# A hybrid retention, sparse-attention and mixture-of-experts layer: experts in order of load, fourteen of them as raw fp32 products on two 64-column tiles

## The reference, cut to what matters

```python
logits = h @ router_w + router_b                 # 512 x 32
top_vals, top_idx = lax.top_k(logits, 4)
gates = softmax(top_vals)
# for every expert e, over the rows (tokens) that chose it:
gu = xb @ w_gu[e] + b_gu[e]                      # 1024 -> 2048
gate, up = jnp.split(gu, 2, axis=-1)
gate = jnp.minimum(gate, 7.0); up = jnp.clip(up, -7.0, 7.0)
glu = gate * jax.nn.sigmoid(1.702 * gate)
y = ((up + 1.0) * glu) @ w_down[e] + b_down[e]   # 1024 -> 1024
# out = x + g2 * segment_sum(y * gate_of_row, token)
```

## Time and profile before

| | us |
|---|---|
| time, median of 3 runs (lowest to highest) | 1501.27 (1499.06 to 1501.77) |
| span of the profiled execution | 1494.1 |
| PE busy | 1459.7 (98%) |
| DVE busy | 1257.1 (84%) |
| ACT busy | 1062.7 (71%) |
| POOL busy | 375.6 (25%) |
| DMA, mean over the span | 318 GB/s |

### The profile page before, as it was taken

One profiled execution on the slowest core, in us unless ns is written; L12 is line 12 of the kernel. 1 busy time (PEld: TensorE's weight loads), 2 busy tenths in 40 slices (PEclk: granted clock), 3 DMA queues, 4 the chain that ended last, 5 costly groups with the idle time before them and its releaser, 6 DMA issues.

```text
span 1494.1 us, 21340 instructions
## 1 busy us (share of the span) xinstructions
PE 1459.7 (98%) x7139; PEld 1149.1 (77%) x7139; DVE 1257.1 (84%) x1146; ACT 1062.7 (71%) x1122; POOL 375.6 (25%) x267
## 2 busy tenths in 40 slices
PE   4999999999999999999999999999999999999997
PEld 1667974567888888888888888888888888888885
DVE  0576765358999999999999999999999999999997
ACT  3542334546887888788888888888788888888883
POOL 1000020203122233322223333222223332222251
PEclk9999999999999999999999999999999999999999
DMA  9655620066899999999999999999999999999994
GB/s 347 214 160 203 223 103 15 27 233 250 344 375 369 375 368 373 370 368 373 371 377 383 370 383 376 372 364 371 374 369 379 373 370 369 377 372 372 384 369 151
DMA packets 95076, 474.96 MB, mean 318 GB/s; under 512 B 23748, under 2 KB 33964, under 8 KB 42816
## 3 DMA queue, kind: packets, MB, share of 16 engines
q1 hardware_dynamic: 82656, 451.39, 78.0%
q0 software_dynamic: 12304, 22.97, 5.5%
q10 hardware_dynamic: 80, 0.13, 0.0%
HBM read 468.16 MB, written 23.09 MB: 329 GB/s over the span
## 4 chain that ended last, share of the span: by engine, by line
PE 92%; DMA 3%; ACT 2%; DVE 1%; issue 0%; SPq 0%; DVEq 0%; ACTq 0%
PE bank L1587 16%; PE bank L1590 15%; PE bank L1594 15%; PE bank L1615 7%; PE bank L1623 7%; PE bank L1616 7%; PE bank L1389 4%; PE bank L1201 3%; PE bank L1203 3%; PE bank L1202 3%; DMA area<-bias_g_parts 2%; PE bank L1563 2%; PE bank L1555 2%; PE bank L1156 1%; PE bank L1362 1%; PE bank L1579 1%
## 5 line engine op out<-in xcount | busy, mean ns | idle before, releaser
L1812 DVE TENSOR_TENSOR e_lo<-ring,e_hi 128x2048 fp32r<-128x2048 f32 x384 | 865.7, 2288 | 62.2 <-ACT e_hi L808 61.3
L808 ACT ACTIVATE e_hi<-ring 128x2048 fp32r<-128x2048 f32 x384 | 728.1, 1920 | 208.3 <-PE bank L1594 207.1
L1587 PE MATMUL bank<-e_hi,x_hi 128*128 128x512 f32 x1024 | 403.7, 394 | 0.0
L1590 PE MATMUL bank<-e_hi,x_lo 128*128 128x512 f32 x1024 | 399.5, 390 | 0.0
L1594 PE MATMUL bank<-e_lo,x_hi 128*128 128x512 f32 x1024 | 274.1, 390 | 0.0
L1587 PEld LDWEIGHTS bank<-e_hi,x_hi 128*128 128x128 f32 x1024 | 192.3, 188 | 46.5 <-issue 7.2
L1594 PEld LDWEIGHTS bank<-e_lo,x_hi 128*128 128x128 f32 x1024 | 192.4, 188 | 40.3
L1590 PEld LDWEIGHTS bank<-e_hi,x_lo 128*128 128x128 f32 x1024 | 192.5, 188 | 39.0
L1615 PE MATMUL bank<-e_hi,act_hi 128*128 128x512 f32 x496 | 196.3, 396 | 0.0
L1616 PE MATMUL bank<-e_hi,act_lo 128*128 128x512 f32 x496 | 193.5, 390 | 0.0
L741 POOL COPY future<-routes 128x1 int32 (+1 forms) x31 | 81.6, 2631 | 366.8 <-DVE area L2116 366.8
(11 more groups left out here) (270 smaller groups left out, 1575.1 us busy)
## 6 DMA issues: line engine op xcount, KB each, us to landing
ring<-in_w_gu SPq DMA_DIRECT2D x256, 1024.0 KB, 9.0
ring<-in_w_down SPq DMA_DIRECT2D x128, 1024.0 KB, 7.2
ring<-in_ada_w SPq DMA_DIRECT2D x24, 1024.0 KB, 9.1
ring<-in_w_in SPq DMA_DIRECT2D x9, 1024.0 KB, 7.9
ring<-in_w_o SPq DMA_DIRECT2D x4, 1024.0 KB, 5.8
xs<-in_x SPq DMA_DIRECT2D x4, 512.0 KB, 4.7
ring<-in_w_in SPq DMA_DIRECT2D x8, 256.0 KB, 5.6
xn_rows<-area POOLq DMA_DIRECT2D x4, 512.0 KB, 5.0
```

What stands on the lines that cost most here:

```text
L808: return nc.scalar.activation(dst, src, ACT.Copy, scale=scale)
L1587: pe.matmul(bank[b][:], x_hi[:, c, :], hi, start=False, stop=False)
L1590: pe.matmul(bank[b][:], x_lo[:, c, :], hi, start=False, stop=False)
L1812: tt(e_lo[c % PARTS][:], raw(period.raw_slot(c)), e_hi[:, c % PARTS, :].bitcast(F32), ALU.subtract).then_inc(lo_ready, 1)
```

## The change

An order of wide (H) and narrow (L) items is written down, and the experts are put into it by load, on the chip.

- Experts 0 and 1 stay first and wide. DVE ranks the other thirty by their count (seven small steps and some more on the tables), PE picks the row lists by rank, SP reads the expert's number of each item from SBUF (TENSOR_LOAD) for its addresses. SP waits for tables_ready before the w_down chunks of expert 0. The 16 heaviest of the thirty are wide, the 14 lightest narrow. Rows of a narrow item past 64 would go to the branch for further items; with the counts above there are none.
- A wide item is computed as before.
- A narrow item takes the raw chunk as it lands: no `hi`, no `lo`. A stationary operand has 64 columns; of two 512-column products one goes to PSUM partitions 0 to 63 and one to 64 to 127 (two column tiles). A w_gu or w_down chunk is 4 fp32 matmuls of 512 columns in place of 12 fp32r ones. A slot of a narrow item is free when PE has used it (chunk_used). The gelu, clip and multiply handle 512 columns instead of 1024, the activations need 4 transposes instead of 8, and ACT moves the upper half of the down sums to partitions 0 to 63 (upper_rows) before rows_out.
- A semaphore bias_used makes SP wait until the bias before was read. The place of up_bias, behind chunk 4, stays.
- The hardware loops over items 2 to 30 are written out on PE, ACT, DVE and SP.

```diff
+ORDER = "HH" + "LHLHLHHLHLHLHHLHLHLHHLHLHHLHLL"
+NARROW = 64
...
             def raw_free(period, c):
 
-                sp.wait_ge(lo_ready, period.at(c) - (SLOTS - 1))
+                before = period.at(c) - SLOTS
+                if isinstance(before, int) and before < MAIN_CHUNKS and not chunk_wide(before):
+                    sp.wait_ge(chunk_used, before + 1)
+                else:
+                    sp.wait_ge(lo_ready, splits_before(before) + 1)
...
-            def up_bias(e):
-
+            def up_bias(i, e):
+
+                if i is not 0:
+                    sp.wait_ge(bias_used, i)
                 for g in range(4):
                     sp.dma_start(bias_g[32 * g:32 * g + 3, :], bias_g_dram[g, e, :, :]).then_inc(g_rows_in, 16)
...
-            def steady(i, e, e_before):
+            def gate_up_chunks(i, e):
                 period = Later(i)
                 for c in range(GU):
                     raw_free(period, c)
                     gu_chunk(period, c, e)
                     if c == 4:
-                        up_bias(e)
+                        up_bias(i, e)
+
+            def down_chunks(i, e_before):
+                period = Later(i)
                 for q in range(DN):
                     raw_free(period, GU + q)
                     down_chunk(period, GU + q, q, e_before)
...
+            e_before, e = 0, 1
+            for i in range(1, E):
+                gate_up_chunks(i, e)
+                if i == 1:
+                    sp.wait_ge(tables_ready, 1)
+                if i + 1 < E:
+                    e_next = sp.value_load(expert_at[0:1, i + 1:i + 2], min_val=0, max_val=E - 1)
+                down_chunks(i, e_before)
+                e_before, e = e, e_next
...
+            def upper_rows(i):
+
+                if not wide(i - 1):
+                    a.wait_ge(chunk_used, Later(i).at(CHUNKS))
+                    copy(upper[0:NARROW, :], bank[4][NARROW:P, :]).then_inc(upper_moved, 1)
...
+            def gate_up_narrow(period):
+
+                i = period.i
+                pe.wait_ge(g_rows_in, i * 64 + 64)
+                pe.wait_ge(xt_taken, i * 2 + 2)
+                pe.wait_ge(up_ready, i)
+                pe.wait_ge(glu_ready, i)
+                for g in range(4):
+                    rows, half = slice(32 * g, 32 * g + 3), slice(NARROW * (g % 2), NARROW * (g % 2) + NARROW)
+                    mm = pe.matmul(bank[g // 2][half, :], ones_b[rows, 0:NARROW], bias_g[rows, :], start=True,
+                                   stop=False)
+                mm.then_inc(bias_used, 1)
+                for c in range(GU):
+                    pe.wait_ge(*period.landed(c))
+                    w = raw(period.raw_slot(c))
+                    for g in range(4):
+                        half = slice(NARROW * (g % 2), NARROW * (g % 2) + NARROW)
+                        mm = pe.matmul(bank[g // 2][half, :], xgT[:, c, 0:NARROW], w[:, 512 * g:512 * g + 512],
+                                       start=False, stop=(c == GU - 1))
+                    mm.then_inc(chunk_used, 1)
+
+            def down_narrow(period, c0, out, turned, between=None):
+
+                i = period.i
+                pe.wait_ge(y_ready, i)
+                pe.wait_ge(ahi_ready, i * 2)
+                for n in range(DN):
+                    pe.wait_ge(*period.landed(c0 + n))
+                    w = raw(period.raw_slot(c0 + n))
+                    for k in range(2):
+                        left = turned[:, 2 * (n % 2) + k, NARROW * (n // 2):NARROW * (n // 2) + NARROW]
+                        for q in range(2):
+                            mm = pe.matmul(out[NARROW * q:NARROW * q + NARROW, :], left,
+                                           w[:, k * D + q * 512:k * D + q * 512 + 512],
+                                           start=(n == 0 and k == 0), stop=(n == DN - 1 and k == 1))
+                    mm.then_inc(chunk_used, 1)
...
-                gate_up(period)
+                if isinstance(i, int) and not wide(i):
+                    gate_up_narrow(period)
+                else:
+                    gate_up(period)
...
+            def order_experts():
+
+                e = slice(0, E)
+                v.wait_ge(order_consts, 1)
+                done(stt(out=load[e, :], in0=dbank(D_["c3"])[e, E:2 * E], scalar=float(E), in1=tie[e, :], op0=ALU.mult,
+                         op1=ALU.add))
+                done(tt(ahead[e, :], load[e, :], ident[e, 0:E], ALU.mult))
+                done(nc.vector.tensor_reduce(my_load[e, :], ahead[e, :], AX.X, ALU.add))
+                done(ts(ahead[e, :], load[e, :], my_load[e, :], None, ALU.is_gt))
+                done(nc.vector.tensor_reduce(my_rank[e, :], ahead[e, :], AX.X, ALU.add))
+                done(ts(chosen[e, :], load_rank[e, :], my_rank[e, :], None, ALU.is_equal))
+                done(ts(is_narrow[e, :], my_rank[e, :], float(N_WIDE), None, ALU.is_ge))
...
+            def mixed(i):
+
                 period, after = Later(i), Later(i + 1)
-                lo(period, 4)
-                lo(period, 5)
-                act_rest(i)
-                for c in range(6, CHUNKS - 1):
-                    lo(period, c)
+                if wide(i):
+                    lo(period, 4)
+                    lo(period, 5)
+                if wide(i - 1):
+                    act_rest(i)
```

More of the change, by code:

```diff
@@ L99, with wide, chunk_wide, splits_before @@
 BESIDE = [1 if 4 <= i < STEPS else 2 if i >= STEPS else 0 for i in range(STEPS + VALUE_LAG)]
+ORDER = "HH" + "LHLHLHHLHLHLHHLHLHLHHLHLHHLHLL"
+NARROW = 64
+assert len(ORDER) == E and ORDER[:2] == "HH" and ORDER[-1] == "L"
+N_WIDE = ORDER.count("H")
+N_NARROW = E - N_WIDE
+assert (N_WIDE - 1) * (CAP + 1) > S * K
+LOAD_RANK = [ORDER[:p].count("H") if m == "H" else N_WIDE + ORDER[:p].count("L") for p, m in enumerate(ORDER)]
+def wide(i):
+    return i >= E or ORDER[i] == "H"
+def chunk_wide(n):
+    i, c = divmod(n + DN, CHUNKS)
+    if n < GU:
+        return wide(0)
+    return wide(i) if i < E and c < GU else wide(i - 1)
+MAIN_CHUNKS = CHUNKS * E
+SPLIT_CHUNKS = [n for n in range(MAIN_CHUNKS) if chunk_wide(n)]
+RAW_CHUNKS = MAIN_CHUNKS - len(SPLIT_CHUNKS)
+def splits_before(n):
+    if isinstance(n, int) and n < MAIN_CHUNKS:
+        return sum(m < n for m in SPLIT_CHUNKS)
+    return n - RAW_CHUNKS
+def wides_before(i):
+    return ORDER[:i].count("H") if isinstance(i, int) and i <= E else i - N_NARROW
+def narrows_before(i):
+    return ORDER[:i].count("L")
 SPLIT_EVERY = 3
@@ L190, in build @@
         ys = view(12288, D)
+        upper = view(15360, 512)
+        last_upper = view(13824, 512)
+        actT = view(5632, 4, P)
+        load, ahead, chosen = view(15264, E), view(15296, E), view(15328, E)
+        is_narrow, my_rank, my_load = view(15880, 1), view(15881, 1), view(15882, 1)
+        beyond = view(15888, NARROW)
         sg = view(13312, D)
@@ L756, in opening @@
             def opening(i):
+                if i == 0:
+                    pool.wait_ge(tables_ready, 1)
                 bring(i, slice(i + 2, i + 3))
@@ L1022, in act_parts @@
                     a.wait_ge(at_full, i * 2 + (half - 1))
+                    if isinstance(i, int) and not wide(i - 1):
+                        copy(actT[:, 2 * half:2 * half + 2, :],
+                             bank[6 + half][:, 0:256].rearrange("p (k n) -> p k n", k=2)).then_inc(ahi_ready, 1)
+                        continue
                     copy(act_hi[:, 4 * half:4 * half + 4, :],
@@ L1455, in counts @@
                 dfree(j)
+                if t == T - 1:
+                    pe.wait_ge(hot_ready, T)
+                    for u in range(T):
+                        pe.matmul(dbank(j)[:, E:2 * E], ones[:], hot32[:, u, :], start=(u == 0), stop=(u == T - 1))
                 for u in range(t + 1):
@@ new lines, in down_narrow @@
+            def down_narrow(period, c0, out, turned, between=None):
[5 more added lines that the diff above has]
+                    w = raw(period.raw_slot(c0 + n))
+                    for k in range(2):
+                        left = turned[:, 2 * (n % 2) + k, NARROW * (n // 2):NARROW * (n // 2) + NARROW]
[4 more added lines that the diff above has]
+                    mm.then_inc(chunk_used, 1)
+                    if between is not None and n == 2:
+                        between()
@@ L1703, in _ @@
             steady(1)
-            with pe.Fori(2, E - 1) as i:
+            for i in range(2, E - 1):
                 steady(i)
@@ L2115, in rows_out @@
                     v.wait_ge(scattered, (i - 1) * 16)
+                if isinstance(i, int) and not wide(i - 1):
+                    narrow_rows(ys, bank[4], upper, gate, narrows_before(i))
+                    return
                 stt(out=ys, in0=banks[:, 2048:3072], scalar=gate, in1=g2_row, op0=ALU.mult,
```

217 lines of the change are left out of this document (128 added, 89 removed).

## The result

| | before | after |
|---|---|---|
| median of the runs, us | 1500.98 (1499.06 to 1501.77) | 1578.64 (1575.14 to 1582.18) |
| ratio, 95% interval | | 1.0529 [1.0506, 1.0552] |
| profiled span, us | 1494.1 | 1577.6 |
| mean granted clock over the span | 0.996 | 0.932 |
| mean period between gate_up starts, items 1 to 31, us | 35.18 | 37.95 |

The changed kernel is 5.3% slower. The forecast was 1543 us: the direction was right, the size was 36 us short. A period is always the time from one bias group on PE (the start S of a gate_up) to the next.

What follows compares the result with a forecast made beforehand. PE was taken to set the 35.12 us period, with the DMA stream nearly full. Span 1494.1 + 19 (periods) + 30 (clock) - 9 (end) + 1.5 (opening) = 1535.6, plus 7.2 to the median: 1543 us, range 1466 to 1590.

Steps and rivals of the forecast that it cites:

- The mechanism: Expert stage: late slots thin the weight stream, and PE waits for the bias at nearly every gate_up start; periods 35 to 36 us or more.
- PE's own work: Expert stage: by PE's work alone, a narrow/wide pair of periods would take 29 and 33 us.
- rival D: Narrow chunks: the two tiles do not overlap with 512 columns, a chunk takes 3.68 us; near 1631 us, chance 0.04.
- The clock, +30: Expert stage: PE gaps before starts drop the clock to half; +30 us (0 to 55), part covered by gathers and scatters.
- the 47 of "all passed on": Clock term's maximum: 14 narrow starts at 2.1 us and 12 wide at 1.5, 47 us if all delay is passed on.
- Rival A: Expert stage: same slots and bias, but the clock does not fall; 1513 us, chance 0.19.
- The refill: Wide period after a narrow one: chunk 2 lands at S+30.1, chunks 3 and 4 follow, then the bias; period 36.1 to 36.7 us.
- the bounds of +19: Expert stage: sum over 30 periods, 1072.8 against 1053.6 us, before the clock term; +19, bounds given as -9 and +40.
- The end: Last item: last landing at S+32 and program end at S+55, against 64.3 us now; -9 us (-14 to -4).
- The opening: Before the stage: DVE ranking, table steps and SP's wait for tables_ready partly reach PE; +1.5 us (0 to 5).
- Rival B: Expert stage: the stream stays full, each period 33.7 us; 1451 us, chance 0.21.
- Rival C: Expert stage: the stream is already at its 373 GB/s ceiling, periods stay 35.1 us, only the end gains; 1494 us, chance 0.07.

Runs made afterwards that it cites:

- Experiments 1: Changed kernel, with each bias (items 2 to 31) issued behind down chunk 2 of the item ahead: 1461.27 us, ratio 0.9765 to the kernel before.
- 9: Changed kernel, with the bias issued behind gate_up chunk 1 of its own item in place of chunk 4: 1461.49 us, ratio 0.9747 to the kernel before.
- 4: Changed kernel, with 31 full-width items and one narrow one at the end, no alternation: 1496.0 us, ratio 0.9987 to the kernel before.
- Experiment 2: Changed kernel, with 22 unused matmuls (fillers) ahead of each gate_up's bias matmul, items 2 to 31: 1559.66 us, ratio 1.0414 to the kernel before.
- no gather: Changed kernel, with the gather of the next item's token rows bounded at row 0: 1544.06 us, ratio 1.0304 to the kernel before.

## Why the prediction was right, and short

*The mechanism* stood as recorded: late slots, the bias behind chunk 4, PE idle before each start. Experiments 1 and 9 show that the bias is what pins the starts, and 4 that the stage loses nothing by the ordering and the written-out loops: the cost comes with the narrow items among the wide ones. One part of it was not so: PE is idle before 25 of the 30 starts, not before all. (PE's own work was put too high, at 29 and 33 us; the terms give 28 and 31.4, and 31.40 is what the wide periods took with the bias early.) A narrow chunk is 5.33/3 = 1.78 us and, with the clock up, 7.04/4 = 1.76, for 1.84; rival D is out. With the clock held up by fillers, the slot for chunk 2 of the next item comes free at S+25.24 in each of the twelve wide periods behind a narrow one (forecast S+25.2), and chunk 6 goes out at S+2.39 in each narrow one (S+2.5).

*The sizes.* 30 periods took 1138.5 us. The forecast's 1072.8 had 30 for the clock on top, so 36 are missing. Each period is split at its first late slot:

| | forecast | after | fillers | no gather |
|---|---|---|---|---|
| wide after narrow: S to slot | 25.2 | 27.42 | 25.24 | 26.89 |
| slot to the next start | 11.1 | 12.13 | 12.15 | 10.85 |
| narrow: S to slot | 2.5 | 3.53 | 2.39 | 3.58 |
| slot to the next start | 32.9 | 33.41 | 33.87 | 32.10 |

*The clock, +30, "part of it is covered"*: this step was too small. The slots come 2.2 us late twelve times and 1.03 thirteen times, 40 us. In a wide period behind a narrow item this is passed on in full, for the start that follows hangs on the slot by a fixed distance (12.13 and, with the clock up, 12.15). The second of two wide items takes 1.5 us more than the forecast's 35.4 four times, 6 more: for it the forecast had no term of the clock. In the 4 us behind such a start, at 645.18, the granted clock was 0.56; its period is 36.7 us, and 35.11 in the run with the bias early, where PE does not wait. So the clock costs 46 us.

That this is so near the 47 of "all passed on" is partly luck: a wide start lost 2.2 us and not 1.5, a narrow start after a wait lost 1.9, near the forecast's 2.1, but five of the thirteen had no wait, and their slot comes at S+2.4 at full clock. Experiment 2 finds 35 by its own count, because in narrow periods its fillers push the next start back by 0.5 us.

Nor does the gap take gathers and scatters in for free, the reason I gave. Rival A (the clock stays up) falls with the 0.62 and 0.52 in the windows. The Trainium skill, TensorE: Matmul & The Clock Gate, section "HAM oscillation — how this bites in real kernels", would have taken the 47 in full; the runs agree with it at the starts that PE waited for, and the stage as a whole reads 0.91.

*The refill, "chunks 3 and 4 5.0 to 5.6 later, 1 for the bias"*, was the other step too small, in the wide period behind a narrow item: slot to next start 11.1 us. It gave the refill to the chunks alone. Without the gather it is 10.85, near the forecast; with it 12.13. In the trace quoted, chunk 2 landed 5.2 us after its issue, but chunk 3 after 8.0 and chunk 4 after 8.8, with POOL's two transfers in between. Over the twelve, chunk 4 lands 6.5 us after chunk 2 and not 5.0 to 5.6, and the start follows it by 0.5 us and not 1: two errors, of which the smaller hides part of the larger. That is 12 x 1.03 = 12 us. The narrow periods add 13 x 0.5 = 7, which no run splits further. The first wide period behind a wide one took 36.06 for 35.4, as it did before (36.05): 1 us. Altogether (40 + 6 - 30) + 12 + 7 + 1 = 36. (I had counted 14, 12 and 4 periods for 13, 12 and 5; at 35.4 for both that changes nothing. And the bounds of +19 should read -12 and +41, not -9 and +40.)

*The end* gave 3.9 us, not 9. The last load:

```profile
1525.65 12.35 SPq L573 DMA_DIRECT2D ring<-in_w_down  x8
```

```profile
DMA to landing us min/median/max: 14.4/14.4/14.4
```

Its last chunk, issued at 1537.7, landed after 14.4 us, at S+34.9 for S+32, and the program ended 25.5 us later for 22. *The opening* cost 4.3, not 1.5. Together 8 us of the span; 36 + 8, less 2 since 30 periods of before are 1055.3 and not 1053.6, is the 42 by which 1577.6 lies over 1535.6. The forecast time misses by 36 only because its last term, 7.2 us from the span to the median of the runs, came out at 1.0; this hides 6 us of the miss, and it is luck.

*Rival B* (the stream stays full, 1451) wasn't what happened, but named the price of the pin: with the bias early the periods are 33.95 us for its 33.7, and the time 1461. *Rival C* falls with the same run: 386 GB/s over 800 us is above the 373 of before. The Trainium skill, DMA: Bandwidth & Descriptors, section "Where 436 GB/s comes from", lets HBM bind at about 358 GB/s per core; this run is 8% above that, so the measurement decides against it for one core running alone.

Left open: how the gather's cost splits between its bytes on the engines and the landing order; whether a seventh slot would let narrow and wide periods share their slack. Neither was tried. Open too is what the order of ACT's work costs in narrow periods once the bias is early.

## What to carry to other kernels

Before work is taken off the bounding engine, list each transfer that the engine needs at a fixed point, with its margin, small ones first. A 3 KB transfer behind 1 MB chunks is as late as they are, and its margin here was so small that three starts of the kernel before already waited for it; issued three places earlier it is free. Compute taken off an engine also takes away the slots' rhythm and the clock: look for the place at which the queue runs dry, and price everything that shares the refill.

## What the runs showed of the hardware

- Two 64-column tiles of fp32 products with 512 columns run fully side by side: four products in 1.76 us, against 0.92 for a full-width one.
- A full queue delivers more but later: load chunks land after a median of 11.7 us at 386 GB/s, and of 7.8 us at 347 GB/s. The two rows (600 to 1400 us, loads of w_gu, early bias first):

```profile
DMA to landing us min/median/max: 5.1/11.7/13.9
```

```profile
DMA to landing us min/median/max: 4.7/7.8/14.2
```

- After some 6 us of idle PE in a dense stage the windows of 4 us read 0.62 and 0.52. Read in windows of 2 us, the clock is 0.75, 0.50, 0.50 and 0.54 from 832 to 840 us: it falls before PE starts again at 834.23 and stays at 1.2 GHz for most of the 6 us behind. With the bias early the granted clock is 0.98 by itself. Fillers bring it to 0.99 with the bias late or early, and where PE has work they cost what they last.
